# Attention outputs times the reciprocal row sums: on VectorE instead of GpSimd

## What is computed

```
s = einsum('bhqd,bhkd->bhqk', q, k) * scale
s = s + c[:, :, q0:q1, None] - c[:, :, None, :q1]
s = where(mask, s, -inf)
p = softmax(s, axis=-1)            # exp(s - max) / row sum
o = einsum('bhqk,bhkd->bhqd', p, v)
mix = o.reshape(B, S, D_MODEL) @ w_o
```

## Time and profile before

| | |
|---|---|
| median of 3 runs | 2243.31 us (2241.97 to 2243.39) |
| profiled execution, time | 2243.55 us |
| profiled execution, span from first to last instruction | 2241.7 us |
| busy share of the span: PE, PEld | 98%, 82% |
| DVE, ACT, POOL | 75%, 53%, 16% |
| eight attention pairs | about 1030 to 1511 us of the span, some 61 us each |

### The profile page before, as it was taken

The page is one execution under the profiler, slowest core; times in us unless marked ns, Lnnn a source line. Parts: engine busy times, 40 slices in busy tenths (PEclk is TensorE's granted clock), DMA queues, the critical chain, the costliest instruction groups (busy, mean ns, idle before and its releaser), DMA issues.

```text
span 2241.7 us, 28950 instructions
## 1 busy us (share of the span) xinstructions
PE 2208.1 (98%) x10409; PEld 1836.7 (82%) x10409; DVE 1676.7 (75%) x2345; ACT 1182.8 (53%) x1871; POOL 362.8 (16%) x353
## 2 busy tenths in 40 slices
PE   8999999999999999999999999999999999999998
PEld 6788878788888888878888888888888888888886
DVE  7676778787777777778666676684767888888866
ACT  5543566255555555356666666663535555555525
POOL 4000000022222222011111111102102222222210
PEclk9999999999999999999999999999999999999999
DMA  5110301366666666430111111132135666666662
GB/s 151 48 56 28 94 1 38 132 131 132 126 126 129 124 127 125 148 114 25 34 39 38 38 38 30 32 104 61 57 132 101 127 129 128 129 129 127 128 170 85
DMA packets 208829, 207.85 MB, mean 93 GB/s; under 512 B 9689, under 2 KB 153281, under 8 KB 208705
## 3 DMA queue, kind: packets, MB, share of 16 engines
q0 software_dynamic: 39168, 75.51, 20.5%
q1 hardware_dynamic: 167808, 126.43, 19.0%
q10 hardware_dynamic: 1728, 4.31, 0.8%
HBM read 122.28 MB, written 83.95 MB: 92 GB/s over the span
## 4 chain that ended last, share of the span: by engine, by line
PE 89%; DVE 7%; ACT 2%; issue 1%; DMA 0%; ACTq 0%; DVEq 0%
PE ps L1208 37%; PE ps L1040 15%; PE ps L1296 14%; PE ps L1408 10%; PE ps L1453 3%; PE ps L1542 3%; PE ps L1440 3%; PE ps L1421 1%; PE ps L1420 1%; DVE rxl L2228 1%; PE ps L1521 1%; DVE resid L2248 1%; DVE sq_ffn L2682 0%; PE ps L1380 0%; DVE xl L2232 0%
## 5 line engine op out<-in xcount | busy, mean ns | idle before, releaser
L968 POOL DMA_DIRECT2D spill<-c x256 | 223.6, 925 | 728.5 <-DVE c L2618 489.5
L2487 DVE TENSOR_TENSOR ring_l<-raw_ffn,ring_h 128x512 fp32r<-128x512 f32 x320 | 222.6, 697 | 154.3 <-ACT ring_h L1769 152.9
L1769 ACT ACTIVATE ring_h<-raw_ffn 128x512 fp32r<-128x512 f32 x320 | 199.1, 626 | 200.3 <-PE ps L1208 104.7
L1862 ACT ACTIVATE c<-ps 128x512 f32<-128x512 f32 x256 | 150.4, 598 | 13.1
L2107 ACT ACTIVATE probs<-ps,nmax 128x896 f32<-128x896 f32 (+7 forms) x128 | 95.1, 743 | 101.6 <-DVE nmax L3023 99.8
L1408 PE MATMUL ps<-xh,wh_att 128*128 128x512 f32 x368 | 148.5, 404 | 0.0
L1769 ACT ACTIVATE ring_h<-w_sum 128x512 fp32r<-128x512 f32 x112 | 69.5, 625 | 146.6 <-PE ps L1040 38.9
L1408 PE MATMUL ps<-xh,wl_att 128*128 128x512 f32 x368 | 144.0, 391 | 0.0
L1408 PE MATMUL ps<-xl,wh_att 128*128 128x512 f32 x368 | 143.9, 391 | 0.0
L3030 DVE TENSOR_TENSOR ptl<-ps,pth 128x512 fp32r<-128x512 f32 (+1 forms) x160 | 96.8, 634 | 52.7 <-ACT pth L2142 51.5
L2618 DVE TENSOR_TENSOR c<-ps,c 128x512 f32<-128x512 f32 x192 | 123.4, 683 | 4.9 <-PE ps L1296 4.5
(11 more groups left out here) (400 smaller groups left out, 6310.1 us busy)
## 6 DMA issues: line engine op xcount, KB each, us to landing
spill<-c POOLq DMA_DIRECT2D x256, 256.0 KB, 5.8
raw_ffn<-in_w_ffn_in SPq DMA_DIRECT2D x88, 512.0 KB, 5.4
raw_ffn<-in_w_ffn_out SPq DMA_DIRECT2D x44, 512.0 KB, 7.5
resid<-spill SPq DMA_DIRECT2D x24, 512.0 KB, 6.8
raw<-in_w_rec_in SPq DMA_DIRECT2D x16, 512.0 KB, 5.6
spill<-resid POOLq DMA_DIRECT2D x16, 512.0 KB, 2.9
raw_att<-in_w_kvf SPq DMA_DIRECT2D x16, 512.0 KB, 4.0
xin<-in_x SPq DMA_DIRECT2D x4, 1024.0 KB, 9.9
```

What stands on the lines that cost most here:

```text
L968: pool.dma_start(spill[m, :, half * BANK:(half + 1) * BANK], block[:, :], accum_op=ALU.add).then_inc(sem, 16)
L1769: act.activation(F.ring_h[slot][:, :], src, ACT.Copy).then_inc(F.unit_hi, 1)
L1862: act.activation(dst[:, :], y if what == "s5" else w, ACT.Copy).then_inc(out_tapped, 1)
L2487: dve.tensor_tensor(F.ring_l[slot][:, :], src, F.ring_h[slot][:, :].bitcast(F32), ALU.subtract).then_inc(F.unit_lo, 1)
```

## The change

The multiplication leaves POOL for DVE in pairs 1 to 7 (for the outputs of pairs 0 to 6). In pairs 1 to 6, DVE does it behind step V0 of unit 0, that is between the low parts of T3 and the maxima of S1. In pair 7 it does it behind step S1 of the pair's start, between the weight split and the first `low_o`. It waits for the same two semaphores as POOL did. POOL's call in pair 7 is gone; the multiplication of pair 7's own outputs stays on POOL.

```diff
@@ pool_pair
                 if with_p:
                     pool.wait_ge(o_added, i * UNITS + 1)
-                if not (isinstance(i, int) and i == 0):
-                    scale_o(i - 1)
                 if with_p:
                     gain_piece(uses["Q"], GAIN["Q"])
@@ gpsimd block
             pool_pair(PAIRS - 2, att_uses(None, last, 1))
-            pool_pair(PAIRS - 1, att_uses(PAIRS - 1, None, 1), with_p=False)
             scale_o(PAIRS - 1)
@@ vector block, pair
                     if not with_p and (u, step) in OUT_LO_AT:
                         split_lo(pieces.use("attE", OUT_LO_AT[u, step]))
+                    if not is_first(i) and (u, step) == ((0, "V0") if with_p else (-1, "S1")):
+                        dve.wait_ge(rinv_loaded, i * 32)
+                        dve.wait_ge(o_added, i * UNITS)
+                        dve.tensor_tensor(resid[:, i - 1, :], resid[:, i - 1, :], rinv[:, :],
+                                          ALU.mult).then_inc(o_scaled, 1)
                     if not with_p:
                         for n in LOW_O_AT.get((u, step), ()):
                             low_o(n)
```

## The result

| | before | after |
|---|---|---|
| median | 2241.94 us (14 runs, 2240.45 to 2243.43) | 2247.12 us (14 runs, 2245.94 to 2248.61) |
| ratio | | 1.0024, 95% interval 1.0015 to 1.0032 |
| profiled execution, span | 2241.7 us | 2246.3 us |

The kernel is slower, by 5.2 us in the medians and by 5.4 us by the ratio (interval 3.4 to 7.2). The forecast was 2249.3, that is + 5.77 on the profiled execution.

A forecast was written before the change was run, and what follows sets the result against it. The prediction took PE, busy for 98% of the span, to set the pace. 2243.55 (profiled execution) + 6.84 for pairs 1 to 6 - 1.07 for pair 7 = 2249.3 us, range 2246.0 to 2252.0.

The forecast's parts named there:

- rival B: Pairs 1 to 6: PE gets back half of the 1.14 us as small gaps close; 2245.9 us, chance 0.06.
- No slack ahead of T0: Unit 1's T0 on PE waits for DVE's S1 maxima through ACT; zero slack, T0 already 0.17 us late.
- The 0.03 us of idle time: PE's idle time in a 60.9 us middle pair, taken to mean that PE cannot catch up later in the pair.
- 1.14 us per pair, six times, 6.84: Pairs 1 to 6: DVE's multiplication delays the S1 maxima, ACT and PE's T0 by 1.14 us each; + 6.84 us.
- Two waits for nothing: The new DVE instruction's two semaphore waits are already met where it stands; cost nothing.
- POOL's removal gives nothing in the middle pairs: Pairs 1 to 6: POOL loses 2.40 us of work, but DVE gets no faster without it; 0.
- - 1.07 us in pair 7: Pair 7: without POOL's multiplication DVE's low part is not held, so drain L3009 is earlier; - 1.07 us, ends 0 and -1.54.
- Rival A: Pairs 1 to 6: DVE's idle time takes up the delay of S1, only pair 7's gain stays; 2242.5 us, chance 0.09.
- C: Middle pairs: DVE is late at a second place too, T0 of unit 2; 2256.2 us, chance 0.04.
- D: Middle pairs: POOL holds DVE there too, by 2.2 us, so removing it gives more back; 2236.1 us, chance 0.02.

The follow-up runs named there:

- the half dose: Against the changed kernel: in pairs 1 to 6 DVE multiplies columns 0 to 511 behind S1 of the pair's start, the rest behind V0 of unit 0; 2243.69 us, ratio 1.0005.
- waits_only: Against the kernel before: only the change's two waits added on DVE in pairs 1 to 6 behind V0 of unit 0, POOL still multiplies; 2241.10 us, ratio 0.9996.
- behind_s1: Against the changed kernel: in pairs 1 to 6 DVE multiplies behind the maxima of S1 of unit 0 instead of ahead of them; 2240.05 us, repeated 2240.87.
- at_start: Against the changed kernel: in pairs 1 to 6 DVE multiplies behind S1 of the pair's start, as in pair 7; 2240.20 us, ratio 0.9990.
- pool_early: Against the kernel before: in pairs 1 to 6 POOL's multiplication starts after the first maxima of the pair's start, beside DVE's weight split; 2242.57 us, ratio 1.0001.
- pool_beside: Against the changed kernel: POOL's multiplication of the Q weights starts after the low part of T2 of unit 0, beside DVE's new multiplication; 2266.92 us, ratio 1.0107.
- mid_only: Against the changed kernel: DVE multiplies only in pairs 1 to 6, POOL multiplies in pair 7 as before; 2248.41 us, ratio 1.0024.

## Why the prediction was right

- **The distance was right, the absolute time in part by luck.** Forecast + 5.77 us, measured + 5.2 in the medians. But 2247.12 lies below the range of the forecast itself (2247.5 to 2252); it is inside the stated range only because the lower end was taken down to 2246.0 for rival B, which did not happen. It also lies below the border of 2248.0 that I had set for "slower". The reason is the starting point: the profiled execution, 2243.55, is longer than each of the 14 runs of before (median 2241.94).
- **No slack ahead of T0: held.** It was read from a distance of 0.29 us from the accumulator read to T0, the same in each pair, and from a load 0.17 us late. After the change the distance is 0.29 again, and the half dose cost its full 0.60. The 0.03 us of idle time, on which I put that PE cannot catch up, were a weak ground: they do not even hold the 0.17 us that I had found, since the rows of matmuls overlap. That it cannot catch up is shown by the pairs, which grew from 60.60 to 61.72 us, by as much as the wait.
- **1.14 us per pair, six times, 6.84: measured 6 x 1.12 = 6.7.** The start-to-start distance was 1.13 at this place. It was right not to use the full 1.22 of the row.
- **Two waits for nothing: held** (waits_only).
- **POOL's removal gives nothing in the middle pairs: held.** With the multiplication at a place on DVE where it is hidden (behind_s1, at_start), a middle pair takes 60.6 us, as with POOL's multiplication in it (before, from pair 2 on). Moving it on POOL (pool_early) changes nothing either.
- **- 1.07 us in pair 7: measured - 1.09**, by the mechanism named. The Trainium skill (GPSIMD Engine Reference, Specifications) states contention of GpSimd with VectorE instructions that have two SBUF inputs. By that rule, the trace agrees in three kernels (3.43, 2.81 and 2.79 us instead of 1.22), and the instructions with a PSUM operand beside them are unchanged.
- **Left out: 0.33 us in pair 2.** The sum was + 5.77; the waits of the traces give 6.72 - 1.09 - 0.33 = 5.30, and the ruler 5.34. I had called PE's idle time in a middle pair 0.03 us from pair 3 alone; one listed wait in pair 2 was outside that stretch. It hangs on DVE's queue and no reading of the old trace would have said that it goes away.
- **Rival A, hidden,** was the one to fear, and it is what behind_s1 and at_start do: 2240 to 2241, against 2242.5 worked out, or 2241.1 from the lower median of before. The place decided, not DVE's share. B, C and D did not show: no gap closed, no second wait, no relief from POOL.

## What to carry over

Before adding work to an engine that is idle for a third of the time, look at what stands right behind the insertion point and who waits for it: the distance between the last release and the start of the waiting instruction, the same in every repetition, shows a path without slack even when no wait is listed. Here one step further down the same queue turns + 5.2 us into - 1 to - 2. And in these traces POOL's multiplications held DVE only where they met an instruction with two SBUF operands, and that one (128x1024) then ended 1.08 us behind POOL's.

## What I had not expected

PE's granted clock in pool_beside. Busy time by stretch, pair 3 (length, PE, PEld, DVE, ACT, POOL, then the clock as a share of full speed):

```profile
1235.50:1238.20 2.70, 0.09 (x1) 0.00 (x0) 2.08 (x3) 0.56 (x2) 0.60 (x1) 1.00 0.00 0
1238.20:1239.20 1.00, 0.92 (x5) 0.87 (x6) 0.42 (x1) 0.74 (x2) 0.00 (x0) 0.85 0.00 0
1239.20:1240.20 1.00, 1.00 (x5) 0.84 (x4) 0.83 (x2) 0.13 (x1) 0.00 (x0) 0.50 0.00 0
...
1242.20:1243.20 1.00, 1.00 (x7) 0.88 (x6) 0.04 (x1) 0.93 (x2) 0.00 (x0) 0.94 0.00 0
1243.20:1244.20 1.00, 1.00 (x6) 0.76 (x5) 0.00 (x0) 0.45 (x2) 0.00 (x0) 1.00 0.00 0
```

After 2.70 us without a matmul PE starts again at the full 2.4 GHz, falls to half of it, 1.2 GHz, within the first microsecond (the share of 0.85 puts it at about 1238.9), and is back some 3.4 us later (the share of 0.94, at about 1242.3). Matmuls of 512 columns start 0.43 us apart in between, where they start 0.23 apart at full clock:

```profile
1240.97 0.63 PE L1405 MATMUL ps<-xh,wh_att 128*128 128x512 f32 x1
1241.40 0.63 PE L1405 MATMUL ps<-xl,wh_att 128*128 128x512 f32 x1
...
1243.44 0.40 PE L1405 MATMUL ps<-xh,wh_att 128*128 128x512 f32 x1
1243.68 0.39 PE L1405 MATMUL ps<-xl,wh_att 128*128 128x512 f32 x1
```

Half clock for 3.4 us would cost a PE that never waits 1.7 us, an estimate from these shares. So it is enough for the 1.50 us per pair that the wait does not explain, nearly as much again as the longer wait itself. The other five middle pairs show the same fall. After the idle times of 1.12 us in the changed kernel, and of 1.54 us in pair 7 of the kernel before, the clock stays at 1.00. Stretches right behind the one of the changed kernel, and then behind the one of the kernel before:

```profile
1230.20:1231.20 1.00, 0.97 (x7) 0.91 (x8) 0.42 (x1) 0.75 (x2) 0.02 (x1) 1.00 0.00 0
1231.20:1233.20 2.00, 2.00 (x15) 1.78 (x14) 1.89 (x4) 0.58 (x2) 1.87 (x1) 1.00 0.00 0
```

```profile
1464.10:1465.10 1.00, 0.99 (x10) 1.00 (x10) 1.00 (x2) 0.00 (x0) 0.00 (x0) 1.00 0.00 0
1466.10:1469.50 3.40, 3.16 (x21) 2.62 (x20) 3.18 (x7) 2.59 (x7) 0.00 (x0) 1.00 0.00 0
```

So a stall on this path was not paid in proportion: the first 1.1 us cost 1.1, the next 1.6 cost 3.1. The length of the idle time alone does not tell whether the clock falls. In layer 0 PE waits for DVE until 314.02 us in the kernel before, for 2.44 us, and until 314.01 in mid_only, for 2.45. The clock falls behind the one and not behind the other (stretch 310 to 318 us, before and then mid_only):

```profile
310.00:318.00 8.00, 5.56 (x17) 4.11 (x17) 5.08 (x6) 1.06 (x1) 0.00 (x0) 0.79 0.00 0
```

```profile
310.00:318.00 8.00, 5.55 (x24) 4.24 (x23) 6.12 (x7) 2.08 (x3) 0.00 (x0) 1.00 0.00 0
```

The change does not touch layer 0; such places are why the ruler is used beside the whole time. What decides between the two is open here.
